# Two passes over the eight chunks in the groups that begin a stage

## The reference

```python
for i in range(DEPTH):                       # DEPTH = 2
    h = rms_norm(x, g_pre_mix[i])
    z = h @ w_in[i]                          # 1024 x 2208
    ...                                      # latent attention, short convolution
    x = x + rms_norm(mix @ w_out[i], g_post_mix[i])

    hm = rms_norm(x, g_pre_mlp[i])
    f = jnp.square(jax.nn.relu(hm @ w_mlp_up[i])) @ w_mlp_down[i]      # D_FF = 4096
    x = x + rms_norm(f, g_post_mlp[i])

    gate = jax.nn.sigmoid(rms_norm(x, g_pre_ple[i]) @ w_ple_gate[i])
    e = p[i] @ w_ple_proj[i]
    x = x + rms_norm(gate * e, g_post_ple[i])
```

## Time and profile before

| | |
|---|---|
| median of 3 runs | 3142.2 us (3139.89 to 3142.69) |
| span of the profiled execution | 3140.4 us |
| PE busy with products | 2937.6 us, 94% of the span, 13824 instructions |
| DVE busy | 1721.0 us, 55% |
| ACT busy | 1175.9 us, 37% |
| POOL busy | 377.8 us, 12% |

### The profile page before, as it was taken

How to read it: one execution, slowest core, us unless ns; L and a number is a source line. 1 busy time by engine, 2 the same in 40 slices (tenths; PEclk the granted TensorE clock), 3 DMA queues, 4 the chain that set the end, 5 groups by cost and what they waited for, 6 DMA issues and landing times.

```text
span 3140.4 us, 38553 instructions
## 1 busy us (share of the span) xinstructions
PE 2937.6 (94%) x13824; PEld 2408.4 (77%) x13824; DVE 1721.0 (55%) x2220; ACT 1175.9 (37%) x1773; POOL 377.8 (12%) x260
## 2 busy tenths in 40 slices
PE   6999999989999999997889999999799999999883
PEld 5777888767888888875677788887588888888663
DVE  5357666364444444457645576671844444444757
ACT  3326666442121212135423366673421212111444
POOL 2220000040000000023313200001300000000423
PEclk9999999999999999999899999999899999999997
DMA  5110000611111111111122100024111111111111
GB/s 190 48 60 31 19 18 18 228 34 41 53 40 51 42 53 51 42 54 34 54 80 67 58 16 23 19 94 151 41 40 48 46 53 47 46 40 53 47 41 67
DMA packets 57872, 175.96 MB, mean 56 GB/s; under 512 B 6176, under 2 KB 6176, under 8 KB 57760
## 3 DMA queue, kind: packets, MB, share of 16 engines
q1 hardware_dynamic: 57760, 174.54, 16.8%
HBM read 149.35 MB, written 29.36 MB: 57 GB/s over the span
## 4 chain that ended last, share of the span: by engine, by line
PE 83%; DVE 9%; issue 4%; ACT 3%; DMA 0%; POOL 0%; DVEq 0%; ACTq 0%; SPq 0%; POOLq 0%
PE ps L575 26%; PE ps L576 26%; PE ps L577 26%; PE ps L736 3%; DVE xf L1326 3%; DVE hl L1319 2%; DVE wl L1301 1%; PE ps L696 1%; PE ps L771 1%; DVE xf L1329 0%; ACT pth L960 0%; ACT wh L960 0%; DVE ptl L1480 0%; PE ps L638 0%; DMA xf<-x_in 0%
## 5 line engine op out<-in xcount | busy, mean ns | idle before, releaser
L575 PE MATMUL ps<-hh,wh 128*128 128x512 f32 x2192 | 877.4, 400 | 69.2 <-DVE wl L1301 27.7
L576 PE MATMUL ps<-hl,wh 128*128 128x512 f32 x2192 | 862.0, 393 | 0.0
L577 PE MATMUL ps<-hh,wl 128*128 128x512 f32 x2192 | 860.6, 393 | 0.0
L575 PEld LDWEIGHTS ps<-hh,wh 128*128 128x128 f32 x2192 | 416.7, 190 | 174.1 <-issue 63.0
L576 PEld LDWEIGHTS ps<-hl,wh 128*128 128x128 f32 x2192 | 416.6, 190 | 93.7 <-issue 7.5
L577 PEld LDWEIGHTS ps<-hh,wl 128*128 128x128 f32 x2192 | 416.1, 190 | 88.4
L575 PE MATMUL ps<-gh,wh 128*128 128x512 f32 x1088 | 436.8, 401 | 37.0 <-ACT xf L960 18.8
L1580 DVE TENSOR_TENSOR xf<-xf,ps 128x512 f32<-128x512 f32 x496 | 334.7, 685 | 185.3 <-PE ps L577 183.2
L577 PE MATMUL ps<-gh,wl 128*128 128x512 f32 x1088 | 433.7, 399 | 0.0
L576 PE MATMUL ps<-gl,wh 128*128 128x512 f32 x1088 | 433.7, 399 | 0.0
L1658 POOL TENSOR_TENSOR accy<-accy,sq 128x512 f32<-128x512 f32 x96 | 134.4, 1400 | 2313.9 <-ACT sq L981 2310.5
(11 more groups left out here) (129 smaller groups left out, 3508.7 us busy)
## 6 DMA issues: line engine op xcount, KB each, us to landing
raw<-w_units SPq DMA_DIRECT2D x204, 512.0 KB, 3.3
hh<-mix_hi SPq DMA_DIRECT2D x16, 512.0 KB, 6.2
hl<-mix_lo SPq DMA_DIRECT2D x16, 512.0 KB, 7.1
xf<-out SPq DMA_DIRECT2D x4, 2048.0 KB, 12.3
out<-xf SPq DMA_DIRECT2D x8, 1024.0 KB, 4.2
stage<-w_head SPq DMA_DIRECT2D x16, 320.0 KB, 2.9
xf<-x_in SPq DMA_DIRECT2D x4, 1024.0 KB, 8.9
out<-x_in SPq DMA_DIRECT2D x4, 1024.0 KB, 15.2
```

The costliest lines, as they stand in the source:

```text
L575: nc.tensor.matmul(dst, ah, bh, start=start, stop=False)
L576: nc.tensor.matmul(dst, ah, bl, start=False, stop=False)
L577: return nc.tensor.matmul(dst, al, bh, start=False, stop=stop)
```

## The change

`side_by_side` now goes through the chunks twice. In the first pass it makes of every chunk the high by high product of each output, and waits only for `pre_hi`, and at the first chunk for each unit's `w_hi`. In the second pass it makes the two products with a low part, and waits for `pre_lo` and, at the first chunk, for `w_lo`. The number of products, their sizes and their banks are the same. The waits for the weight units that stood ahead of the calls are now inside. `pre_ready` stays for `unit_output`.

```diff
-            def side_by_side(outputs, t, ready, done):
+            def side_by_side(L, units, banks, t, R, done):
 
                 for k in range(DC):
-                    ready(k)
-                    for bank, slot in outputs:
-                        last = split_product(ps[:, bank, :], wh[:, slot, k, :], wl[:, slot, k, :],
-                                             hh[:, k, hs(t)], hl[:, k, hs(t)], k == 0, k == DC - 1)
+                    pe.wait_ge(pre_hi, R * 16 + t * 8 + k + 1)
+                    for w, bank in zip(units, banks):
+                        if k == 0:
+                            pe.wait_ge(w_hi, L * UNITS + w + 1)
+                        nc.tensor.matmul(ps[:, bank, :], wh[:, w % SLOTS, k, :], hh[:, k, hs(t)], start=k == 0, stop=False)
+                for k in range(DC):
+                    pe.wait_ge(pre_lo, R * 16 + t * 8 + k + 1)
+                    for w, bank in zip(units, banks):
+                        if k == 0:
+                            unit_ready(L, w)
+                        nc.tensor.matmul(ps[:, bank, :], wh[:, w % SLOTS, k, :], hl[:, k, hs(t)], start=False, stop=False)
+                        last = nc.tensor.matmul(ps[:, bank, :], wl[:, w % SLOTS, k, :], hh[:, k, hs(t)],
+                                                start=False, stop=k == DC - 1)
                         if k == DC - 1:
                             last.then_inc(done, 1)
@@
-                for n in range(SLOTS):
-                    unit_ready(L, n)
-                side_by_side([(n, n) for n in range(SLOTS)], 0, pre_ready(R, 0), in_out)
+                side_by_side(L, range(SLOTS), range(SLOTS), 0, R, in_out)
@@
-                for i in range(2):
-                    unit_ready(L, M_AT + i)
-                side_by_side([(i, (M_AT + i) % SLOTS) for i in range(2)], 0, pre_ready(R, 0), up_out)
+                side_by_side(L, (M_AT, M_AT + 1), (0, 1), 0, R, up_out)
                 pre_stats(L, 0, 0)
-                side_by_side([(2 + i, (M_AT + i) % SLOTS) for i in range(2)], 1, pre_ready(R, 1), up_out)
+                side_by_side(L, (M_AT, M_AT + 1), (2, 3), 1, R, up_out)
@@
                 for n in range(2):
-                    unit_ready(L, G_AT + n)
                     pe.wait_ge(e_copy, L * 16 + 5 + n)
-                side_by_side([(n, (G_AT + n) % SLOTS) for n in range(2)], 0, pre_ready(pre_at(L, 1), 0), gate_out)
+                side_by_side(L, (G_AT, G_AT + 1), (0, 1), 0, pre_at(L, 1), gate_out)
```

## The result

The changed kernel takes 3150.05 us in the median of 12 runs (3147.66 to 3152.07), the kernel before 3142.76 us in 12 runs beside it (3139.89 to 3145.52): ratio 1.0023, 95% interval 1.0015 to 1.0032. It is slower by 7.3 us, or 0.23%, with 4.7 to 10.1 us in the interval. The forecast was +8.9 us.

The account below looks back on a forecast made before the run. PE, busy for 94% of the span, was taken as the bound. The span, 3140.4 - 4.7 + 6.1 + 6.1 + 1.4 = 3149.3 us, is +8.9; on the median of 3142.2 that gives 3151.1 us, range 3147.8 to 3153.3.

Parts of the forecast that it names:

- The start in the first layer: First layer's input stage: products go on from 17.2 us instead of waiting until 21.23, a gain of 4.7 us.
- The second layer's start: Second layer's input stage: starts some 4 us sooner, covered by output n = 4's 9.89 us wait for `zr`; nothing.
- Up's first half and the gate: Up stage's first half and gate, both layers: PE comes late to both, so the end stays; nothing.
- Up's second half: Up stage's second half: 34 products behind the last high part, partly at the low clock; a loss of 6.1 us each layer.
- The low clock behind the copy: First layer, behind PE's wait for DVE's copy: about seven products at the low clock, a loss of 1.4 us, once.
- Rival A: Up's second half: the clock stays up in the first pass, 3.8 us lost in each layer; 3145.1 us, chance 0.12.
- Rival B: Up's second half: loss covered by ACT's slack, and both layers' starts count; 3132.8 us, chance 0.04 with its half.
- C: Up stage and later waits: more low clock, up to 10.5 us lost in each layer; 3156 us the middle, chance 0.09.
- D: Program's start: transfers of `x` and weights come in another order, so the start brings nothing; 3155.8 us, chance 0.04.

Follow-up runs that it names:

- e2: The kernel before with two passes only in the input stage's group, in both layers: 3137.05 us against 3143.40.
- e3: The kernel before with two passes only in the up stage's first half and the gate's group: 3144.01 us against 3143.40.
- e1: The kernel before with two passes only in the up stage's second half: 3156.11 us against 3143.40.
- e4: The changed kernel with the up stage's second half put back to one pass: 3138.09 us against 3143.40 for the kernel before.
- e8: The kernel before, still one pass, with the input group's waits for low weight parts moved ahead of each unit's products: 3140.81 us against 3142.69.
- e5: The changed kernel with four unused products ahead of the waits for chunks 4 to 7 in up's second half: 3149.94 us, kernel before 3142.69.
- e9: The changed kernel with seven unused products ahead of the waits for chunks 4 to 7 in up's second half: 3148.75 us, kernel before 3141.92.
- e10: The changed kernel itself, measured and profiled once more: 3149.33 us against 3141.92 for the kernel before.
- e6: The changed kernel with low products four chunks behind the high ones in up's second half: 3139.56 us against 3142.69 for the kernel before.
- the lagged kernels: The changed kernel with low products four chunks, or one, behind the high ones in up's second half: 3139.56 and 3139.41 us.

## Why the prediction was right, point by point

**The start in the first layer** was put at 4.7 us; the first pair of profiles gives 4.52, the mean of all of them 4.9. It was kept whole across the wait for ACT and DVE, as argued.

**The second layer's start** was put at nothing, covered by 9.89 us of waiting for `zr`: confirmed by 14.82 us of waiting in the changed kernel and 15.02 in e2. The group started 5.3 us sooner, not some 4, and the cover took that too.

**Up's first half and the gate** were put at nothing: e3, +0.6 us in the timing with zero inside its interval, and both groups as long as before in its trace.

**Up's second half** was put at 6.1 us a layer. It was 5.84 and 5.85, and e1 and e4 show that no other call loses. Its parts: the 34 products, forecast at 10.1 us, took 9.77 and 9.78, since some 10 of them and not 11.7 ran at the low clock; of the delay 1.05 us were covered and not 1.08. The forecast took its 5.0 us of low clock from stretches elsewhere and let them begin at the last high part. But the clock fell within the first pass, and how much of the low stretch came to lie behind the last high part follows from nothing in the working; that it was so near is partly luck. It was 4.1 to 4.8 us in the four up stages of the changed kernel's two profiles.

**The low clock behind the copy** is the term whose reasoning was weakest. I had it as 1.4 us once: the first layer waited 1.48 us, the second 3.03. The changed kernel waits 3.06 and 3.09 us (forecast 3.5), and the first layer's lead shrank from 2.07 us at that product to 0.50 us at the end of the MLP (1413.47 against 1413.97), so 1.6 us. But which layers of the old form pay is chance: e3 waits 1.50 and 1.49, e2 3.03 and 1.48, e4 3.04 and 1.48, e8 1.49 and 3.03. In the earlier trace rows, and in the five other layers that wait some 1.5 us, the low clock falls into `down`'s first 24 products and is hidden by the wait; in the four that wait 3 us it falls behind the wait, and PE pays. The old form pays in four of the ten layers in these profiles, the two passes in all ten (the changed kernel, e1, e5, e9, e10), so the price is better put at 1.6 us in each layer times the six in ten that change, some 1.9 us. A long wait isn't enough for it: e6 waits 3.10 us in both layers and pays in the first alone. So that this term came out near the forecast is in part luck.

**The sum.** With the measured terms it is -4.5 + 5.84 + 5.85 + 1.6 = +8.8 us; the profile shows +6.1. The kernel before lost another 3.4 us (7.91 less 4.52) ahead of the first up stage, to the low clock stretches that it happened to have there, and the changed kernel 0.7 us behind the second layer's copy wait (6.1 less 5.35, its lag at that product). So forecast and profile are nearer in their parts than in their totals. The medians say +7.3 and +7.4; the single parts (e1 +12.7, e2 -6.4, e3 +0.6) add up to +6.9. The range's upper end, 3153.3 us, doesn't follow from the prediction's own ends, which give 3142.2 + 6.5 + 6.5 + 1.8 - 4.0 = 3153.0; nothing hangs on the difference.

**Rival A** (the clock stays up in the first pass) fell: granted clock 0.50 for the first 4.2 us of the 34 products, in both layers of the changed kernel. The strict reading of the Trainium skill ("TensorE: Matmul & The Clock Gate", Part 1, the low clock after an idle window) doesn't hold here: PE was never idle for more than 2.96 us in that pass, and the clock fell; e9 shows it falling in one layer with gaps of 1.8 us at most in front. But the evidence that the forecast had for it was thin. It was one row, a clock of 0.50 behind 3.45 us in which PE was busy for 1.39. The same place in the second layer of the kernel before, with the same busy time, kept the full clock:

```profile
2255.25:2258.70 3.45, 1.39 (x5) 1.00 0.00 0
2258.70:2262.05 3.35, 3.35 (x16) 1.00 0.00 0
```

So the row shows that the clock can fall there, not that it does. In the changed kernel and e1 it fell in all six up stages, which the row didn't promise; that the forecast had it so was a choice between two values that came out well.

**Rival B** (the loss is covered) decides at 1.05 us of delay, as the lagged kernels show, and the changed kernel is at 6.9. **C and D** didn't come.

## What to carry to other kernels

When a consumer is slower than its inputs, work can be split off and done early; when it is faster, work split off is work left for behind the last input, and the price is the amount behind that input less the slack of whoever waits next. Here the same helper met both cases: the first stage's four outputs take PE 2.7 us a chunk against 1.5 us for a low part and gained, up's two outputs take 1.4 us against 3 us and lost. Choosing for each call keeps the gain without the loss: e4, with one pass in up's second half, has the first and an up span as before. And the place of the waits comes first: in e8, still one pass, moving them brought about two thirds of what the start gained. Where another engine is the one waited for behind the group, as in the second layer's input stage, an earlier start brings nothing.

## What the runs showed of the hardware that was not expected

TensorE's clock fell to 1.2 GHz with PE far from idle: in e9 within a microsecond after a stretch in which it was busy 7.19 of 10.4 us in pieces, while the other layer of the same kernel, busy 7.63 of 10.8 us, kept 2.4 GHz. Keeping PE at work in the gaps isn't a sure way to keep the clock, and one profile's total can be some 3 us off another's for that reason alone; times between two events close to each other agreed to 0.1 us where the clock was the same (the up span was 43.85 to 43.90 us in all ten layers of the kernels with one pass there).
